# Stick-breaking attention: the first head's scores put between the two groups of the values' projection, its softplus beside the second group

## What is computed

```python
def stick_breaking_mixer(h, w_qkv, w_out):
    qkv = (h @ w_qkv).reshape(B, S, 3, H, dh).astype(jnp.float32)
    ...
    for blk in range(S // SB_BLOCK):
        ...
        z = jnp.einsum('bhtd,bhsd->bhts', qb, kb) * scale
        strict = s_idx < t_idx
        log_1m = jnp.where(strict, jax.nn.log_sigmoid(-z), 0.0)
        suffix = lax.cumsum(log_1m, axis=3, reverse=True) - log_1m
        a = jnp.where(strict, jnp.exp(jax.nn.log_sigmoid(z) + suffix), 0.0)
        outs.append(jnp.einsum('bhts,bhsd->bhtd', a, vb))
    ...
    return o @ w_out
```

## Time and profile before

| | |
|---|---|
| timed runs | 2530.45, 2526.8, 2529.94 us; median 2529.94 |
| profiled execution | 2518.72 us, its span 2517.4 us |
| mean granted TensorE clock | 0.979 |
| TensorE busy | 2402.9 us (95%) |
| VectorE, ScalarE, GpSimd busy | 1005.8 (40%), 879.3 (35%), 1070.3 us (43%) |
| values' projection | first matmul 921.21, last starts 965.35 us |
| heads | from 968.48 to about 1100 us |

### The profile page before, as it was taken

One profiled execution on the slowest core, in us unless ns is written; L12 is line 12 of the kernel. 1 busy time (PEld: TensorE's weight loads), 2 busy tenths in 40 slices (PEclk: granted clock), 3 DMA queues, 4 the chain that ended last, 5 costly groups with the idle time before them and its releaser, 6 DMA issues.

```text
span 2517.4 us, 31056 instructions
## 1 busy us (share of the span) xinstructions
PE 2402.9 (95%) x12860; PEld 2022.4 (80%) x12860; DVE 1005.8 (40%) x1529; ACT 879.3 (35%) x1275; POOL 1070.3 (43%) x811
## 2 busy tenths in 40 slices
PE   7999999999999999999999999998899989999997
PEld 6766877788888787768777888887888988899886
DVE  3236723622211623736236222115573445744403
ACT  4324523422222414745234232224344223422321
POOL 7423733344454441027433444543344433544452
PEclk9999999999999998999999999998999999999999
DMA  4211421222222221013212222222111221222232
GB/s 154 85 58 59 143 84 51 86 99 92 93 101 99 84 92 42 1 59 134 92 51 84 92 100 93 101 93 92 59 35 68 84 76 68 101 93 92 92 103 73
DMA packets 64012, 211.40 MB, mean 84 GB/s; under 512 B 8832, under 2 KB 13056, under 8 KB 63872
## 3 DMA queue, kind: packets, MB, share of 16 engines
q1 hardware_dynamic: 59120, 206.00, 23.4%
q10 hardware_dynamic: 4752, 3.42, 0.5%
HBM read 207.29 MB, written 2.10 MB: 83 GB/s over the span
## 4 chain that ended last, share of the span: by engine, by line
PE 83%; DVE 11%; ACT 3%; issue 2%; DMA 1%; ACTq 0%; POOL 0%; SPq 0%; DVEq 0%
PE ps L404 68%; PE ps L510 5%; DVE u_lo L1457 2%; DVE x L1472 2%; PE ps L735 1%; PE ps L751 1%; PE ps L756 1%; PE ps L802 1%; DVE arena L1470 1%; PE ps L668 1%; PE ps L769 1%; DVE acc L1507 1%; DMA w_land<-in_units 1%; DVE y_ffn L1470 1%; PE ps L426 1%
## 5 line engine op out<-in xcount | busy, mean ns | idle before, releaser
L2096 POOL TENSOR_TENSOR w_lo<-w_land,w_hi 128x512 fp32r<-128x512 f32 x768 | 1025.2, 1360 | 1349.6 <-ACT w_hi L930 1349.4
L404 PE MATMUL ps<-u_hi,w_hi 128*128 128x512 f32 (+3 forms) x2560 | 827.5, 350 | 45.9 <-DVE u_lo L1457 21.7
L404 PE MATMUL ps<-u_lo,w_hi 128*128 128x512 f32 (+3 forms) x2560 | 820.3, 347 | 0.0
L404 PE MATMUL ps<-u_hi,w_lo 128*128 128x512 f32 (+3 forms) x2560 | 816.8, 346 | 0.0
L404 PEld LDWEIGHTS ps<-u_hi,w_hi 128*128 128x128 f32 x2560 | 460.4, 190 | 122.4 <-DVE u_lo L1457 27.5
L930 ACT ACTIVATE w_hi<-w_land 128x1024 fp32r<-128x1024 f32 x384 | 401.3, 1050 | 333.3 <-DMA w_land<-in_units 326.2
L404 PEld LDWEIGHTS ps<-u_lo,w_hi 128*128 128x128 f32 x2560 | 458.1, 190 | 62.8 <-issue 1.7
L404 PEld LDWEIGHTS ps<-u_hi,w_lo 128*128 128x128 f32 x2560 | 458.3, 190 | 60.1
L404 PE MATMUL ps<-hid_hi,w_hi 128*128 128x512 f32 (+1 forms) x594 | 220.2, 371 | 0.0
L404 PE MATMUL ps<-hid_lo,w_hi 128*128 128x512 f32 (+1 forms) x594 | 219.7, 370 | 0.0
L404 PE MATMUL ps<-hid_hi,w_lo 128*128 128x512 f32 (+1 forms) x594 | 219.4, 369 | 0.0
(11 more groups left out here) (304 smaller groups left out, 2831.2 us busy)
## 6 DMA issues: line engine op xcount, KB each, us to landing
w_land<-in_units SPq DMA_DIRECT2D x384, 512.0 KB, 3.2
x<-in_xT SPq DMA_DIRECT2D x4, 528.0 KB, 7.1
arena<-in_memT ACTq DMA_DIRECT2D x2, 1024.0 KB, 5.2
outT<-x SPq DMA_DIRECT2D x16, 128.0 KB, 1.7
arena<-in_masks ACTq DMA_DIRECT2D x1, 448.0 KB, 3.6
arena<-in_consts ACTq DMA_DIRECT2D x1, 296.0 KB, 4.0
consts<-in_consts SPq DMA_DIRECT2D x1, 256.0 KB, 7.8
arena<-in_consts ACTq DMA_DIRECT2D x1, 256.0 KB
```

Of the source, the lines that this page charges most:

```text
L404: ins = pe.matmul(ps[:, bank, at:at + c1 - c0], w, rhs(k, c0, c1)[which], start=first and h == 0, stop=last and h == 2)
L2096: pool.tensor_tensor(w_lo[:, u % LAND, half], w_land[:, u % LAND, half], w_hi[:, u % RING, half].bitcast(F32), ALU.subtract).then_inc(*uni ...
```

## The change

The first group of the values' projection goes to banks 4 to 7, the second to 3 to 6, and `columns` to bank 0. Behind the first group's fourth unit TensorE does `z(0, 0)`; behind the second group it does `sums(0, 0)` at once, then `z(1, 0)` and `z(0, 1)`. ScalarE writes the constants ahead of the projection, takes Abs, Exp and Ln of the first head right behind its `tokens` of the first group, ahead of the next `hi_to`, and both `weights(0, 0, n)` ahead of the second head's Abs. VectorE does `softplus(0, 0)` between its `tokens` of the two groups. The helper functions of ScalarE are only moved up. No instruction is added or dropped, apart from waits.

```diff
-            def by_token(name, u_, n_blocks, between=()):
-                between = dict(between)
+            def by_token(name, u_, n_blocks, between=(), bank=None):
+                between, bank = dict(between), bank or (lambda g, b: n_blocks * g + b)
                 for g in range(2):
                     for b in range(n_blocks):
-                        await_empty([n_blocks * g + b])
+                        await_empty([bank(g, b)])
...
-                columns("sb", rstd[:, XS], 4, 7)
-                by_token("sb_v", u_tok, 4)
-                await_empty(range(8))
-                pe.wait_ge(*sb_c.at(1))
+                columns("sb", rstd[:, XS], 4, 0)
...
-                z(0, 0)
+                def first_scores():
+                    await_empty([0, 1, 2])
+                    pe.wait_ge(*sb_c.at(1))
+                    z(0, 0)
+
+
+                by_token("sb_v", u_tok, 4, [(3, first_scores)], lambda g, b: 4 - g + b)
+                sums(0, 0)
+                await_empty([3, 4, 5])
                 z(1, 0)
+                await_empty([6, 7])
                 for i in range(SB_H // 2):
                     more = i + 1 < SB_H // 2
-                    sums(0, i)
+                    if i:
+                        sums(0, i)
...
                 table("natural_log_exp_and_others")
+                for n, (name, by) in enumerate((("ones", -1.0), ("neg_suffix", 1.0), ("ident", 1.0))):
+                    act.activation(sums_c[:, n * P:(n + 1) * P], const(name), ACT.Copy, scale=by)
+                for n in range(3):
+                    ins = act.activation(sb_fill[:, n * P:(n + 1) * P], const("neg_suffix"), ACT.Copy, scale=1e30 if n < 2 else 0.0)
+                ins.then_inc(*sb_c.up())
...
                 for j in range(8):
                     hi_to(UNIT["sb_v"] + j + LEAD + 1)
                     if j % 4 == 3:
                         if j == 3:
                             act.wait_ge(*emptied_at["sb", "columns"])
                         for b in (1, 3):
                             tokens("sb_v", b, j // 4, sb_v)
...
+                    if j == 3:
+                        for n in range(2):
+                            absolute(0, 0, n)
+                        for n in range(2):
+                            exponential(0, 0, n)
+                        for n in range(2):
+                            log1p(0, 0, n)
                 for i in range(SB_H // 2):
 
+                    if i == 0:
+                        for n in range(2):
+                            weights(0, i, n)
                     for n in range(2):
                         absolute(1, i, n)
-                    weights(0, i, 0)
+                    if i:
+                        weights(0, i, 0)
                     exponential(1, i, 0)
-                    weights(0, i, 1)
+                    if i:
+                        weights(0, i, 1)
                     exponential(1, i, 1)
...
-                for g in range(2):
-                    for b in (0, 2):
-                        tokens("sb_v", b, g, sb_v)
...
+                for b in (0, 2):
+                    tokens("sb_v", b, 0, sb_v)
                 softplus(0, 0)
+                for b in (0, 2):
+                    tokens("sb_v", b, 1, sb_v)
                 for i in range(SB_H // 2):
                     softplus(1, i)
```

More of the change, by code:

```diff
@@ L509, in by_token @@
                                 for n, (a_, w_) in enumerate(((u_h, w_hi[:, u % RING]), (u_l, w_hi[:, u % RING]), (u_h, w_lo[:, u % LAND]))):
-                                    ins = pe.matmul(ps[:, n_blocks * g + b, :], a_, w_[:, cols],
+                                    ins = pe.matmul(ps[:, bank(g, b), :], a_, w_[:, cols],
                                                     start=k == 0 and n == 0, stop=k == DT - 1 and n == 2)
@@ L515, in by_token @@
                     for b in range(n_blocks):
-                        holds((name, g, b), [n_blocks * g + b], unit_done.at(UNIT[name] + 4 * g + 4))
+                        holds((name, g, b), [bank(g, b)], unit_done.at(UNIT[name] + 4 * g + 4))
             def columns(name, r, n_blocks, bank):
@@ L1241, in stick_breaking @@
                 table("natural_log_exp_and_others")
[L1242 to L1248, removed]
                 for n, (name, by) in enumerate((("ones", -1.0), ("neg_suffix", 1.0), ("ident", 1.0))):
@@ L1286, in out_hi @@
                     act.activation(u_hi[:, i, XS], ps[:, 6 + i % 2, :], ACT.Copy).then_inc(*o_hi_at.up())
[L1288 to L1293, removed]
+                for j in range(8):
+                    hi_to(UNIT["sb_v"] + j + LEAD + 1)
+                    if j % 4 == 3:
+                        if j == 3:
+                            act.wait_ge(*emptied_at["sb", "columns"])
+                        for b in (1, 3):
+                            tokens("sb_v", b, j // 4, sb_v)
+                    if j == 3:
+                        for n in range(2):
[4 more added lines that the diff above has]
+                            log1p(0, 0, n)
                 for i in range(SB_H // 2):
+                    if i == 0:
+                        for n in range(2):
+                            weights(0, i, n)
                     for n in range(2):
                         absolute(1, i, n)
-                    weights(0, i, 0)
+                    if i:
+                        weights(0, i, 0)
                     exponential(1, i, 0)
-                    weights(0, i, 1)
+                    if i:
+                        weights(0, i, 1)
                     exponential(1, i, 1)
```

## The result

The change made the kernel faster, by more than was forecast: a median of 2510.75 us (4 executions, 2505.29 to 2515.49) against 2528.86 us (4 executions), a ratio of 0.9928 with a 95% interval of 0.9906 to 0.995. That is 18.1 us less. Measured twice more, with six executions each, it gave 0.9945 (0.9927 to 0.9963) and 0.9945 (0.993 to 0.996), 13.4 and 14.8 us less. So the gain is some 14 us where 8.8 were forecast, and the median lies under 2517.0, the range's lower end. The profiled execution took 2505.29 us with a span of 2504.0, 13.4 less than the span of before.

A forecast was written before the change was run, and what follows sets the result against it. TensorE, dense over the heads, was held up by four idle gaps and low clock in their opening. 3.04 + 2.9 + 3.04 + 6.05 + 5.4 = 20.43 against 29.21 gave -8.8 us: 2521.1 us, range 2517 to 2526.5.

The forecast's parts named there:

- Steps 1 to 7: The change followed from new banks through the second group to `z(1, 1)`, each part with its price: -8.8 us in all.
- late casts: Softplus delays the casts of the second group's weights and TensorE waits there: up to 6 us, so -2.8; chance 0.03.
- a fall at the boundary between the groups: Clock falls at `z(0, 0)`, part of the second group runs at half: up to 3.4 us, down to -5.4; chance 0.07.
- a slower kernel: New idle drops the clock and the heads never bring it back: +11.2 us, 2541, if some 45 us; chance 0.03.
- The rival without a fall: Clock stays up at the new idle ahead of `sums(1, 0)`: -11.3 us, 2518.6; chance 0.12.
- Step 7: `sums(1, 0)` ends at 14.9 us behind the projection, or 17.4 at low clock; from `z(1, 1)` on the order is as before.
- the sum: From the projection's wait to `z(1, 1)`: 20.43 us after against 29.21 before, so -8.8 us; chance 0.60.
- The cause given for the fall: The new 3.0 us idle ahead of `sums(1, 0)` makes the clock fall, as idles of 2.74 and 2.03 us did before.
- its price: Low clock lasting about as long as `sums(1, 0)`: 5.4 - 2.9 = 2.5 us lost.
- The long low stretch: Clock stays down through `sums(1, 0)`, `z(1, 1)` and `sums(0, 1)`: gain only -4.5 us, 2525.4; chance 0.15.
- `sums` ended both: Argument against the slower rival: both low stretches of the heads' opening, the longest 13.7 us, ended with a `sums` stage.

The follow-up runs named there:

- the filled kernels: Changed kernel plus extra 128-row matmuls, result unread, in the idle gaps of the heads' opening and end: ratios to before 0.9916, 0.9928, 0.9933 and 0.9928.
- undivided extra matmuls: Changed kernel plus 11 unread matmuls all behind `z(0, 1)` and 11 ahead of `sums(1, 7)`: ratios 0.9916 and 0.9928 on 128 rows, 0.992 on 64.

## Why the prediction was wrong

**The plan of the stages was right.** Steps 1 to 7 against the profile: the wait ahead of the projection gone; `z(0, 0)` 2.96 us (3.04), with no wait on either side; the cast of 944.84 pushed to 948.58 (about 949); the first `sp_lo` at 951.8 (952 to 960); `sums(0, 0)` at once and 2.86 us long (2.9); `z(1, 0)` 3.04 (3.04); `sums(1, 0)` 11.81 us behind the projection (12.0), waiting for `sp_lo`; 5.08 us long (5.4); `z(1, 1)` at 16.89 (17.4). The opening became 9.3 us shorter between the two profiles, where 8.8 was forecast. The rivals with late casts, with a fall at the boundary between the groups and with a slower kernel did not come. The rival without a fall (-11.3) is nearest to the measured time, but a fall came in all four profiles of the changed kernel.

**The step that failed** is the last one: that nothing behind `z(1, 1)` would change. Step 7 has "From there the order is that of before" and "the dense stretch unchanged at 92.2 us", and the sum therefore ends at `z(1, 1)`. Up to there it held: 9.3 us less in the mean of four profiles against four, where 8.8 were forecast. Behind it it did not. In two of the four profiles of before the low stretch ran on past `z(1, 1)`, and the way from there to `times_v(0)` took 13.84 and 15.82 us instead of 8.84; in the changed kernel it took 8.84 to 8.87 each time. That is 3.0 us in the mean, and the heads' end adds 1.7: 9.3 + 3.0 + 1.7 = 14.0.

The same error stands in how the profile was set against the median: "that execution lies 11.2 us under the median of the timed runs, 2529.94, and nothing in the gaps depends on it, so I take the 8.8 off the median". Those 11.2 us were low clock, and part of it lay in the very stretch that the change rearranges. The profiled executions of before are 5.1 us longer in the mean than the first of them. By stages that is 3.1 us at the opening, 3.3 ahead of the projection, where both kernels vary alike, and 1.2 less behind `times_v(0)`. The profile's granted clock was 0.979; over 65 timed executions of before it is 0.9752 in the mean, and only 6 reach 0.979. Low time is twice the missing share: 2 x 0.0248 x 2526 = 125 us against 2 x 0.021 x 2517 = 106. The mean over 16 timed executions of the changed kernel is 0.9799, so 101 us. Half of the 24 us between 125 and 101, so 12, is the most that the clock can be of the 14 us gained, as a low clock over an idle gap costs nothing. At the opening TensorE's idle fell from 4.8 to 1.4 us in the mean of four profiles, 3.4 of the 12.3 us; the other 8.9 went with the low clock. The text had the Trainium skill's remark, "TensorE: Matmul & The Clock Gate", Part 1, that the place of the change varies from run to run, and applied it only to the new kernel's loss, where it hardly varied (6.8 to 10.3 us), and not to the old one's (20.6 to 40.9), where it did.

**The heads' end** and its 14.0 - 12.3 = 1.7 us were not in the sum. The same idle of 3.0 us was followed by 10.2, 0, 10.2 and 6.8 low us in before and 0, 6.9, 6.8 and 0 in the changed kernel; whether that is more than chance, eight profiles don't settle.

**The cause given for the fall was wrong**, though its price was nearly right. Step 7 rests on "An idle of 3.0 us will hardly pass without a fall". The clock fell inside `z(0, 1)` in three of four profiles, ahead of the idle, and in the fourth 0.4 us after the idle began; because in the three `z(0, 1)` ran slowly, the idle shrank to 0.7 to 1.2 us. And the idle of 3.0 us at the heads' end passed without a fall three times in eight. The trace of before could have warned: its second low stretch began at 987.3, when the idle of 2.03 us (from 986.88) had lasted 0.4 us. That the price came out, 2.0 to 2.3 us (64.20 to 64.52 us to `z(1, 1)` against 62.18 in the filled kernels) where 2.5 were taken, is in part luck: `sums(1, 0)` waited for `sp_lo` in any case, so the slow `z(0, 1)` cost nothing, and only `sums(1, 0)` at the low clock was paid for.

What is shown: with matmuls on 128 rows in the two gaps no low stretch appeared over the heads in four profiles of four, without them one appeared at the opening in four of four. What is not shown is that the extra work prevents the fall inside `z(0, 1)`. Up to the end of `z(0, 1)` the changed kernel and its kinds with undivided extra matmuls do the same instructions; the clock fell in it in three of four profiles of the changed kernel, in the one with 64 rows, and in neither of the two with 128. Work that comes later can't be the reason, so chance remains a rival for these two. Whether 64 rows matter is open too.

**The long low stretch** was a rival for the changed kernel only. It is a common case of the kernel before: in three of the six profiles that have its order at the opening without extra matmuls (34.2, 37.6 and 40.9 us) the clock did not come back for over 30 us of nearly unbroken work, so "`sums` ended both" was no law but the luck of one trace.

**A version faster than both** is the changed kernel with the extra matmuls: ratios to before of 0.9916, 0.9928, 0.9933 and 0.9928 on 128 rows and 0.992 on 64, against 0.9928, 0.9945 and 0.9945 without them. Between the medians on one chip it is 3.5 to 4.5 us on 128 rows and 7.7 on 64; the intervals touch. On 128 rows its opening is 2.0 to 2.4 us shorter in each profile and `sb_out` comes 2.0 to 4.9 us sooner.

## What to carry to other kernels

Before a profile's gaps are taken off a median, hold its granted clock against that of the timed executions: if they differ, part of the time is in low stretches that this profile didn't show, and the stage that holds the low stretches should be seen in several profiles. A change that removes idle gaps at the head of a dense stage can bring more than the gaps: here the low stretches behind them also became shorter and steadier (6.8 to 10.3 us instead of 20.6 to 40.9), though which part of the change does that is not shown. An order that puts other work over a wait also pays where that wait is new: the banks alone brought a wait of 1.78 us that only the scores between the groups cover.

## What was unexpected of the hardware

- The low clock can go on through work: 40.9 us at 0.50 with 40.4 us busy, while the same stages at full clock, busy for 91.29 of 91.30 us, held 1.00.
- The clock can fall with next to no idle ahead: 2.6 us behind a gap of 0.41 us, and in the changed kernel behind no gap at all; and it can stay at 1.00 over a gap of 3.03 us and behind it.
- A VectorE cast of 128x512 took 0.42 us with GpSimd idle (at 978.17 in the profile of before) and 1.52 us beside its subtractions (at 951.75 in that of the changed kernel).
